# Recurrence gates multiplied ahead of the recurrent attention, ScalarE's chain between its value products, selected attention's loads issued under it

## What is computed

```python
# 1: recurrent attention (mLSTM), 4 heads of 96: q, k, v, output gate, input and forget gates
s   = einsum('bhtd,bhsd->bhts', q, k) * exp(d_log - m_t)
h   = num / maximum(abs(den), exp(-m_t));  h = rmsnorm(h) * gain * sigmoid(output gate)
# 2: gated linear recurrence (RG-LRU), 384 channels, 6 blocks of 64, over a causal convolution x of 4 taps
r, i = sigmoid(x @ w_a + b_a), sigmoid(x @ w_x + b_x)
log_a = -8 * r * softplus(-lam);  a = exp(log_a)
u = sqrt(-expm1(2 * log_a)) * (i * x)
h_t = a_t * h_{t-1} + u_t;  out = h * gelu(g)
# 3: selected attention, 4 heads of 64: each query attends to its 256 best-scored keys
softmax(q k^T / 8 + mask) v
```

## Time and profile before

| | us |
|---|---|
| median of 3 runs | 3240.03 (3236.83 to 3241.76) |
| the profiled execution | 3239.98 |
| its span, first to last instruction | 3238.4 |
| TensorE busy | 3015.8 (93%) |
| VectorE busy | 1597.6 (49%) |
| ScalarE busy | 1195.7 (37%) |
| GpSimd busy | 1042.3 (32%) |
| TensorE, mean granted clock | 0.969 of full |

### The profile page before, as it was taken

How to read it: one execution, slowest core, us unless ns; L and a number is a source line. 1 busy time by engine, 2 the same in 40 slices (tenths; PEclk the granted TensorE clock), 3 DMA queues, 4 the chain that set the end, 5 groups by cost and what they waited for, 6 DMA issues and landing times.

```text
span 3238.4 us, 49889 instructions
## 1 busy us (share of the span) xinstructions
PE 3015.8 (93%) x18148; PEld 2596.6 (80%) x18148; DVE 1597.6 (49%) x3075; ACT 1195.7 (37%) x2173; POOL 1042.3 (32%) x686
## 2 busy tenths in 40 slices
PE   5798976999999999998999999999999889999999
PEld 4487954777888888877999977997896889988877
DVE  2699923723222323123008377981213837878861
ACT  3311136433212221123114356772322637666750
POOL 1132201232322224564225203344331543432325
PEclk9899997899999999999999999999999999999999
DMA  2122241232111112342268533323335762231223
GB/s 96 56 97 96 89 117 39 59 112 104 46 52 45 52 45 79 116 153 107 94 139 258 141 103 79 68 82 117 141 118 185 211 167 63 84 85 40 61 96 129
DMA packets 224150, 325.68 MB, mean 101 GB/s; under 512 B 81318, under 2 KB 167206, under 8 KB 221814
## 3 DMA queue, kind: packets, MB, share of 16 engines
q1 hardware_dynamic: 188838, 277.29, 28.9%
q10 hardware_dynamic: 33360, 39.98, 3.5%
q0 software_dynamic: 1792, 6.29, 0.7%
HBM read 229.95 MB, written 93.57 MB: 100 GB/s over the span
## 4 chain that ended last, share of the span: by engine, by line
PE 71%; DVE 6%; ACT 3%; issue 2%; POOL 2%; DMA 0%; POOLq 0%; DVEq 0%; ACTq 0%
PE psum L474 15%; PE psum L2197 15%; PE psum L2400 7%; PE psum L1986 7%; PE psum L1056 6%; PE psum L1025 6%; PE psum L1036 5%; PE psum L739 2%; PE psum L716 2%; DVE arena L2798 1%; PE psum L728 1%; PE psum L1071 1%; POOL out_ring L1976 1%; PE psum L3136 1%; PE psum L2837 1%
## 5 line engine op out<-in xcount | busy, mean ns | idle before, releaser
L2197 PE MATMUL psum<-parts_ffn 128*128 128x512 f32 x2112 | 482.9, 391 | 3.6 <-DVE parts_ffn L2154 3.6
L2197 PEld LDWEIGHTS psum<-parts_ffn 128*128 128x128 f32 x2112 | 398.8, 189 | 87.4 <-issue 2.2
L474 PE MATMUL psum<-parts_even,parts_ffn 128*128 128x256 f32 x2496 | 306.1, 285 | 5.2 <-DVE parts_ffn L2534 4.0
L474 PEld LDWEIGHTS psum<-parts_even,parts_ffn 128*128 128x128 f32 x2496 | 303.9, 194 | 5.9 <-DVE parts_ffn L2534 4.5
L474 PE MATMUL psum<-parts_odd 128*128 128x248 f32 x2304 | 277.1, 283 | 19.1 <-ACT arena L514 16.7
L474 PEld LDWEIGHTS psum<-parts_odd 128*128 128x128 f32 x2304 | 273.6, 193 | 21.8 <-ACT arena L514 15.6
L2267 DVE SCALAR_TENSOR_TENSOR arena<-psum,arena 128x1023 f32<-128x1023 f32 x88 | 112.9, 1283 | 329.8 <-ACT arena L2251 323.6
L514 ACT ACTIVATE arena<-psum 128x256 f32<-128x256 f32 (+2 forms) x240 | 87.6, 376 | 456.1 <-PE psum L474 451.2
L403 PE MATMUL psum<-parts_mixer 128*128 128x512 f32 x912 | 212.1, 395 | 10.5 <-ACTq L412 10.5
L403 PEld LDWEIGHTS psum<-parts_mixer 128*128 128x128 f32 x912 | 174.5, 192 | 48.3 <-ACTq L412 7.6
L1098 ACT ACTIVATE both<-psum 128x512 fp32r<-128x512 f32 x256 | 140.1, 596 | 108.0 <-PE psum L1036 107.5
(11 more groups left out here) (339 smaller groups left out, 5848.9 us busy)
## 6 DMA issues: line engine op xcount, KB each, us to landing
arena<-ffn_up_b SPq DMA_DIRECT2D x44, 512.0 KB, 3.2
arena<-ffn_down_k SPq DMA_DIRECT2D x44, 512.0 KB, 3.6
arena<-x SPq DMA_DIRECT2D x10, 2048.0 KB, 8.6
arena<-w_in_e SPq DMA_DIRECT2D x13, 1024.0 KB, 6.7
e_tokens<-arena ACTq DMA_DIRECT2D x26, 512.0 KB, 3.1
x<-arena SPq DMA_DIRECT2D x24, 512.0 KB, 5.0
arena<-w_in_o SPq DMA_DIRECT2D x12, 992.0 KB, 6.3
o_tokens<-arena ACTq DMA_DIRECT2D x24, 496.0 KB, 3.0
```

What stands on the lines that cost most here:

```text
L474: last = pe.matmul(self.bank(t), self.hT[:, a, k, t * P:(t + 1) * P], self.weights.parts[:, self.weights.slot(s), b, k, :], start=(k, a, b ...
L2197: last = pe.matmul(self.core.psum[:, 4 * u + 2 * s + h, :], parts[:, s, a, k, :], self.hT[:, b, k, h * HALF:(h + 1) * HALF], start=(k, a, ...
```

## The change

It does the following.

- The gate products (`lru_gates`) and the sigmoids (`sigmoid_pairs`) stand ahead of the recurrent attention, as soon as `tok1`'s sums are taken out; the recurrent attention's TensorE part waits for the sigmoids. `coefficients` moves with them.
- The softplus is split off and stands between `feat1` and `tok1` on ScalarE.
- Exp, Tanh, Sqrt and Gelu, three of each, stand one by one between ScalarE's copies of value products: behind copies 4 to 6 and 12 to 14 of the two rounds. ScalarE's loop over the rounds is written out for that.
- `gate_input` follows the masks on GpSimd.
- `dsa`'s loads wait for the last applied weights of the recurrent attention only. Its q and k lie where the recurrent attention's were, and scores contract over the 64 partitions that hold data, with nothing zeroed.
- The output gates' loads stand in SyncE's queue behind `dsa`'s first loads.
- The pieces in `dsa` stand at other steps.

```diff
-        self.loads_after, self.ahead = after, None
+        self.loads_after, self.ahead, self.before_second = after, None, None
@@ Attention.sync
         for i in range(self.rounds):
+            if i == 1 and self.before_second is not None:
+                self.before_second(sp)
@@ Lru
-    def sigmoids_and_roots(self, act):
-        F = self.F
+    def softplus(self, act):
         link = Chain(act, self.act_order)
 
         link(act.activation(self.t0, self.lam, ACT.Abs))
         link(act.activation(self.t0, self.t0, ACT.Exp, scale=-1.0))
         act.activation(self.t0, self.t0, ACT.Ln, bias=1.0).then_inc(self.coef_ln, 1)
-        for f in range(F):
+
+    def sigmoid_pairs(self, act):
+        for f in range(self.F):
             act.wait_ge(self.gated, f + 1)
             act.activation(self.r[:, f], self.both(f, 0), ACT.Sigmoid, bias=self.b_a[:, f:f + 1]).then_inc(self.sigmoids, 1)
             act.activation(self.i[:, f], self.both(f, 1), ACT.Sigmoid, bias=self.b_x[:, f:f + 1]).then_inc(self.sigmoids, 1)
...
+    def decay(self, act, f):
+        act.wait_ge(self.coef_ready, 2)
+        act.wait_ge(self.sigmoids, 2 * self.F)
+
+        act.wait_ge(self.conved, f + 1)
+        act.activation(self.x[:, f], self.r[:, f], ACT.Exp, scale=self.coef2[:, f:f + 1]).then_inc(self.decayed, 1)
+
+    def half_angle(self, act, f):
+        act.wait_ge(self.decayed, f + 1)
+        act.activation(self.r[:, f], self.r[:, f], ACT.Tanh, scale=self.coef[:, f:f + 1]).then_inc(self.tanhed, 1)
+
+    def root(self, act, f):
+        act.wait_ge(self.tanhed, f + 1)
+        act.activation(self.u[:, f], self.r[:, f], ACT.Sqrt, scale=-4.0).then_inc(self.rooted, 1)
+
+    def gelu(self, act, f):
         act.wait_ge(self.g_loaded, 16)
-        for f in range(F):
-            act.activation(self.g[:, f], self.g[:, f], ACT.Gelu_apprx_tanh).then_inc(self.gelued, 1)
+        act.activation(self.g[:, f], self.g[:, f], ACT.Gelu_apprx_tanh).then_inc(self.gelued, 1)
@@ Mlstm.weigh
                 act.wait_ge(self.summed, N * i + N + n + 1)
-                act.activation(self.num[:, bass.ds(i + 2 * s, 1), t, :].rearrange("p a b -> p (a b)"), ps[:, 4 + n % 4, 0:DH + 1], ACT.Copy).then_inc(self.taken, 1)
+                act.activation(self.num[:, i + 2 * s, t, :], ps[:, 4 + n % 4, 0:DH + 1], ACT.Copy).then_inc(self.taken, 1)
+                if (i, n) in self.between:
+                    self.between[i, n](act)
@@ dense_attention
-    qs, ks, vs = core.take(2, S), core.take(2, S), core.take(2, TT, dv)
-    qp, kp = qs, (ks, ks)
+    qs, ks = core.take(2, S), core.take(2, S)
+    if rest_at is not None:
+        core.parts_top = rest_at
+    vs = core.take(2, TT, dv)
+    qp, kp = qs[0:dq], (ks[0:dq], ks[0:dq])
...
-    zeros = [qs[dq:P].rearrange("p a b -> p (a b)"), ks[dq:P].rearrange("p a b -> p (a b)")] if dq < P and not split else []
+    zeros = []
@@ build
+        softplus_part = add(Part())
...
-            hold(pe, [(mlstm.multiplied, 3 * mlstm.N), (mlstm.taken, 4 + 2 * mlstm.N)])
+            hold(pe, [(mlstm.columns_ready, 1)] + tok1.taken_out + tok1.multiplied)
             lru.make_gates(pe)
 
+        def lru_softplus(act):
+
+            hold(act, scores.done)
+            lru.softplus(act)
+
         def lru_sigmoids(act):
 
-            hold(act, [(mlstm.columns_turned, 1), (mlstm.rows_stored, 16)])
-            lru.sigmoids_and_roots(act)
-
+            hold(act, [(mlstm.columns_turned, 1), (mlstm.rows_stored, 16)] + tok1.weights.raw_free())
+            lru.sigmoid_pairs(act)
...
-            hold(pe, [(mlstm.columns_ready, 1)] + tok1.taken_out)
+            hold(pe, [(mlstm.columns_ready, 1)] + lru.gates_done)
             mlstm.multiply(pe)
 
+        for f in range(lru.F):
+            for i, n, step in ((0, 4 + f, lru.decay), (0, 12 + f, lru.half_angle), (1, 4 + f, lru.root), (1, 12 + f, lru.gelu)):
+                mlstm.between[i, n] = lambda act, f=f, step=step: step(act, f)
+        add(Part(tensor=lru_gates, scalar=lru_sigmoids, vector=lru.coefficients))
         add(Part(sync=mlstm_loads, tensor=mlstm_products, scalar=mlstm.weigh, vector=mlstm.apply_weights, gpsimd=mlstm_masks))
-        add(Part(tensor=lru_gates, scalar=lru_sigmoids, gpsimd=lru.gate_input, vector=lru.coefficients))
-
-        add(Part(sync=mlstm.load_output_gate))
-        vector_pieces = {0: mlstm.divide, 5: mlstm.means, 10: mlstm.normalize}
-        for h in range(mlstm.H):
-            vector_pieces[12 + h] = lambda dve, h=h: mlstm.gate(dve, h)
-        scalar_pieces = {0: mlstm.absolutes, 2: mlstm.output_gates, 3: mlstm.squares, 8: mlstm.roots}
+        add(Part(gpsimd=lru.gate_input))
+
+        vector_pieces = {4: mlstm.divide, 12: mlstm.means, 15: mlstm.normalize}
+        for h, at in enumerate((19, 20, 21, 22)):
+            vector_pieces[at] = lambda dve, h=h: mlstm.gate(dve, h)
+        recurrence_at = (5, 6, 7, 11, 13, 14)
+        scalar_pieces = {3: mlstm.absolutes, 6: mlstm.squares, 8: mlstm.output_gates, 13: mlstm.roots}
...
-            elif at > 0:
-                next(recurrence[0], None)
+            if at in recurrence_at:
+                next(recurrence[0])
...
-        core.top, core.parts_top = core.words, 11 * S
+        core.top, core.parts_top = core.words - 8, mlstm.heads_at
         dsa = dense_attention(core, "dsa", 4, 64, 64, feat[AQ:AQ + 256], feat[AK:AK + 256], tok[:, AV:AV + 256],
                                ds, mlstm.loop_done + choose.done + lru.gates_done, masks=masks, scale=64 ** -0.5,
-                              aside=(dsa_scalar_aside, dsa_vector_aside))
+                              aside=(dsa_scalar_aside, dsa_vector_aside), rest_at=11 * S)
+        assert core.parts_top <= mlstm.ends_at
+        dsa.loads_after = [(mlstm.multiplied, 3 * mlstm.N)]
...
         add(dsa)
+        dsa.before_second = mlstm.load_output_gate
```

More of the change, by code:

```diff
@@ L1278, in sigmoids_and_roots @@
             act.activation(self.i[:, f], self.both(f, 1), ACT.Sigmoid, bias=self.b_x[:, f:f + 1]).then_inc(self.sigmoids, 1)
+    def decay(self, act, f):
         act.wait_ge(self.coef_ready, 2)
-        act.wait_ge(self.sigmoids, 2 * F)
-        for f in range(F):
-            act.wait_ge(self.conved, f + 1)
-            act.activation(self.x[:, f], self.r[:, f], ACT.Exp, scale=self.coef2[:, f:f + 1]).then_inc(self.decayed, 1)
-        act.wait_ge(self.decayed, F)
-        for f in range(F):
-            act.activation(self.r[:, f], self.r[:, f], ACT.Tanh, scale=self.coef[:, f:f + 1]).then_inc(self.tanhed, 1)
-        act.wait_ge(self.tanhed, F)
-        for f in range(F):
-            act.activation(self.u[:, f], self.r[:, f], ACT.Sqrt, scale=-4.0).then_inc(self.rooted, 1)
+        act.wait_ge(self.sigmoids, 2 * self.F)
[8 more added lines that the diff above has]
+    def gelu(self, act, f):
         act.wait_ge(self.g_loaded, 16)
-        for f in range(F):
-            act.activation(self.g[:, f], self.g[:, f], ACT.Gelu_apprx_tanh).then_inc(self.gelued, 1)
+        act.activation(self.g[:, f], self.g[:, f], ACT.Gelu_apprx_tanh).then_inc(self.gelued, 1)
     def coefficients(self, dve):
@@ L1354, in __init__ @@
         self.ready_to_load = []
+        self.between = {}
         s = core.sem
@@ L1383, in place @@
         self.pt = core.take_parts(2, self.offset[TT])
-        core.parts_top = base
+        self.heads_at = base
+        self.den, self.ss = shaped(core.parts[:, base + 4 * S:base + 4 * S + 2 * H * TT], (2, H * TT))[:, 0], shaped(core.parts[:, base + 4 * S:base + 4 * S + 2 * H * TT], (2, H * TT))[:, 1]
+        core.parts_top = self.ends_at = 18 * S
         self.og, self.hn = core.take_parts(H, TT, DH), core.take_parts(H, TT, DH)
         self.sq = shaped(num[:, 0:H * TT * DH], (H, TT, DH))
-        self.den, self.ss = core.take_parts(H * TT), core.take_parts(H * TT)
-        core.parts_top = max(core.parts_top, base + 3 * 2 * S + 2 * TT * (DH + 1))
     def load_gates(self, sp):
@@ L1491, in weigh @@
         act.wait_ge(self.columns_ready, 1)
-        with act.Fori(0, 2) as i:
+        for i in range(2):
             for n in range(N):
@@ L1498, in weigh @@
                 act.wait_ge(self.multiplied, N * i + n + N - 1)
+                at = (i + 2 * s) * TT + j
                 act.activation(self.w[:, n % 2, 0:S - j * P], self.ab[:, s, j * P:S], ACT.Exp,
-                               bias=self.cs[:, bass.ds((i + 2 * s) * TT + j, 1)]).then_inc(self.weighed, 1)
+                               bias=self.cs[:, at:at + 1]).then_inc(self.weighed, 1)
             for n in range(N):
@@ L2575, in dense_attention @@
 def dense_attention(core, name, heads, dq, dv, q, k, v, out_sb, after, masks=None, scale=1.0, kv_of_slot=False,
-                    v_step=None, v_first=0, v_shared=False, aside=(None, None), split=False):
+                    v_step=None, v_first=0, v_shared=False, aside=(None, None), split=False, rest_at=None):
     half = heads // 2
-    qs, ks, vs = core.take(2, S), core.take(2, S), core.take(2, TT, dv)
```

(3 more changed lines are left out.)

1 line of the change is left out of this document (added).

## The result

The changed kernel takes **3269.23 us** (median of 20 executions, 3237.01 to 3277.18) where the kernel before takes 3240.04 (20 executions, 3236.83 to 3246.97). The ratio is 1.008, with a 95% interval of 1.0064 to 1.0096: slower by 29 us, where 29.4 us of gain were forecast. The executions of the changed kernel differ in how long TensorE's clock stays at half: in most of them the mean granted clock is 0.951 to 0.955 and the time 3265 to 3277, in three of them it is 0.961 to 0.965 and the time 3237 to 3249. The profiled execution (3271.28 us, span 3269.7, clock 0.953) is one of the many.

The account below looks back on a forecast made before the run. It took TensorE, busy for 93% of the span, as the bound and sought its idle time. Selected attention starting 25.9 us earlier and itself 3.5 us shorter made 29.4 us: 3239.98 - 29.4 = 3210.6 us, range 3204 to 3219.

Parts of the forecast that it names:

- The scores then contract over 64 partitions, which no row here has ... I take no change.: Selected attention's scores: 64 partitions in place of 128 were taken to cost nothing, from 0.43 us per 512 columns over 96.
- half clock through both rounds: Rival in the selected attention: lightly loaded TensorE lacks full clock even in the second round, +44 us, 3255; chance 0.03 (slower).
- the two are level, so 10.6 us of products leave the path and cost nothing.: Ahead of the recurrent attention: last sigmoid at 435.9, DMA wait before until 436.03, so the moved gate products hide.
- its clock should still be full: Start of the recurrent attention: TensorE stands still only 2.3 us, not 13.51, keeping full clock; gain 1.2 us.
- the forecast's 73.4: Time from the recurrent attention's first score to the selected attention's first score: 73.4 us, where before it was 99.26.
- The rival on SyncE's queue: Early selected-attention loads stand behind something on SyncE's queue, leaving only the ordering: about 3235 to 3240; chance 0.05.
- a chain in front that is late: Rival ahead of the recurrent attention: gates, sigmoids and table together late by 0 to 6 us, 3212 to 3217; chance 0.07.
- ScalarE's chain between the copies, 0.35 us: Recurrent attention's value products: activations and table loads fit between ScalarE's copies, except the last copy comes 0.35 us late.
- Softplus, coefficients, input product: 0: Softplus in ScalarE's idle time between projections, coefficients early, input product on GpSimd under value products: no cost forecast.
- The loads: Selected attention's loads issued about 493.4, head 0 there before 500, start at 509.4 in place of 535.29.
- The table switch at the start: Ahead of the recurrent attention: ScalarE loads Exp's table in 1.28 us after the last sigmoid, first weighting at 437.2.
- The selected attention, 116.2 us: Whole selected attention: 86.5 us without pieces, 26.6 for VectorE pieces, 1.9 and 0.2 on ScalarE, 1 for the clock.

Follow-up runs that it names:

- experiment 4: Changed kernel with scores over 128 partitions (upper 64 zeroed on GpSimd) and the recurrent attention's head loads released ahead of the gate products: 3214.9 us, ratio 0.9918.
- experiment 1: Changed kernel with the selected attention's scores over all 128 partitions, the upper 64 zeroed on GpSimd under the value products: 3225.49 us, ratio 0.9953.
- experiment 2: Kernel before the change with one edit, the selected attention's scores over 64 partitions: 3285.77 us, ratio 1.0126.
- experiment 3: Changed kernel with TensorE releasing the recurrent attention's head loads ahead of the gate products, not behind the sigmoids: 3262.52 us, ratio 1.0059.
- experiment 8: As experiment 4, with three extra products of unused result behind the gate products, in TensorE's wait for the sigmoids: 3212.09 us, ratio 0.9917.
- 6: As experiment 4, with the pieces in the selected attention at the steps of the kernel before: 3212.38 us, ratio 0.9913.
- 5: As experiment 4, but the selected attention's scores contract over 96 partitions, 32 of them zeroed: 3219.03 us, ratio 0.9935.
- experiment 9: As experiment 8, with the pieces in the selected attention at the steps of the kernel before: 3212.38 us, ratio 0.991.

## Why the prediction was wrong

**The step that failed first: "The scores then contract over 64 partitions, which no row here has ... I take no change."** The row it was nearest to, 96 partitions in 0.43 us for 512 columns, is right about one product: at full clock, four products of 256 columns took 1.10 us over 64 partitions (517.42 in the changed kernel) and 1.10 us over 128 (512.49 in experiment 4). The price lay in the clock of the engine, which runs everything else too: 50.0 us in D to O, 48.9 of it undone by experiment 1. The unknown was costed at one value, nothing, with no upper end. The upper end was at hand, in the rival "half clock through both rounds" (+44 us). That rival happened, a little larger (+50), but its condition was another: it was argued from how lightly TensorE is loaded, with the clock of 1.00 from 608.9 against it. That row held for scores over 128 partitions, and the change took just that away. A row of before speaks against a rival only while the change leaves alone what made the row.

The Trainium skill, TensorE: Matmul & The Clock Gate, section Why this matters for your kernels, says that a single matmul over 32 rows takes as long as one over all 128; the two rows of 1.10 us, for 64 and 128, agree. Its Part 1 says that the clock is granted by how busy TensorE is; in experiment 2 TensorE was busy for all of the 70 us from 620 to 690 and was granted 0.50, so here the trace doesn't agree: busy time as the profile counts it wasn't enough.

**The second: "the two are level, so 10.6 us of products leave the path and cost nothing."** The chain itself was sized well: products from 1.67 us after T (forecast 1.7), last sigmoid ended at 433.68, 14.9 us after T (forecast 14.5). The cover was not there. The loads that were to hide it were released by TensorE, from behind the products: 10.2 us lost. The prediction named one condition for the heads, "SyncE can't issue the heads before the projection is stored". In the trace of before the other one, TensorE's release, cost nothing, because TensorE was idle when it gave it. The prediction asked who waits for TensorE's new wait and named only TensorE's own work. Experiment 3 gave back 8.5 us of it, experiment 4 9.4.

**The third, a small one: "its clock should still be full".** In experiment 4 TensorE stood still for 2.60 us; the clock fell 0.2 us before it resumed and stayed at 0.50 for 6.7 us behind that. The mean of 0.68 over 14.6 us was read as leaving "the full clock for the first 5 us of it", which is right for the kernel before. But there the clock fell 4.1 us after TensorE had stopped, and in experiments 3 and 4 it fell 2.3 and 2.5 us after, so the 5 us (1.2 of them TensorE's own work) couldn't be carried over. Ahead of the second round some kernels lost it again. The table sets the time of M to D against how long the clock was at half in it, from windows of 0.5 us:

| | wait ahead of round 1, 2 (us) | half clock in round 1, 2 (us) | M to D (us) |
|---|---|---|---|
| 8 | none, 0.55 | 0, 0 | 71.69 |
| 1 | 12.31, 0.53 | 4.0, 0 | 72.93 |
| changed kernel | 12.18, 1.23 | 4.2, 0 | 73.73 |
| 6 | 2.60, 1.29 | 6.8, 0 | 75.08 |
| 3 | 3.50, 1.46 | 5.7, 3.4 | 76.23 |
| 5 | 2.60, 1.49 | 6.8, 3.4 | 76.79 |
| 4 | 2.60, 1.98 | 6.7, 3.4 | 77.24 |

Experiment 9 had no half clock either, and 71.23. So the forecast's 73.4 was too much for a full clock, by 1.7 to 2.2 us (it put the gain of the full clock at 1.2 us; in experiment 8 the value products ended 71.0 us after M, where before it was 73.8). The changed kernel met 73.4 because 4.2 us of half clock and a wait of 1.23 us at the second round made that up: the number came out by luck.

**Slips in its numbers.** The rival on SyncE's queue has a chance of 0.05 and a time of 3235 to 3240, but "within" has 0.03. And a chain in front that is late by 0 us gives 3210.6, not the 3212 at which that rival starts. Neither matters for the outcome.

**What was right.**

- *ScalarE's chain between the copies, 0.35 us.* The second round's 144 value products ran in one piece (16.22 us), the last copy followed 0.03 us behind, and the first score 0.69 us behind the last product. The low end, taken because the gaps were in the rows, was right.
- *Softplus, coefficients, input product: 0.* The input product ran on GpSimd from 500.99, under the value products, and nobody waited for it.
- *The loads:* issued from 501.38, 0.3 us after VectorE's last weights (501.06) and 16.0 us ahead of D, as forecast (493.4 for 509.4), and the first score waits for no DMA. The rival that they stand behind something on SyncE's queue didn't come true.
- *The table switch at the start:* in experiment 4 the last sigmoid ended at 434.80, the load took 1.28 us from 434.82 and the first weighting began at 436.12, 1.32 us after the sigmoid (forecast 1.3). With the clock full, in experiment 8, VectorE's first product came at 438.00, 3.1 us after the last sigmoid, as forecast (435.9 to 439.0); in experiment 4 it waited for TensorE at half clock and came 4.35 us after. The Trainium skill, ScalarE: Activation LUTs, section What ACT_TABLE_LOAD costs, adds a drain to each switch, 1.4 us; the trace doesn't agree, as in experiment 4 there are 0.02 us in front of the load and 0.02 behind it.
- *The selected attention, 116.2 us, with 128 partitions:* 120.86, 119.45 and 118.62 in experiments 1, 4 and 8, and at the old steps 115.79 and 118.20 in 6 and 9. At the steps that the forecast was made for it is thus 2.4 to 4.7 us over; whether that is the rival of the clock in the thin steps isn't shown.
- *The split on GpSimd, 10 us of slack.* In experiment 4 it is freed at 603.69, and with its 18.1 us is done at 621.8, 10.1 ahead of O.

In experiment 9 the whole stretch took 204.98 us, against 204.2 by the forecast's sum. That is near by luck in part: T to M is 0.9 us over the forecast, M to D 2.2 under and D to O 2.0 over, in a kernel with 128 partitions, early heads, three added products and the old steps.

## What to carry to other kernels

When work is put ahead of a wait to hide it, look for who raises the semaphore that starts the transfer waited for: if it is the same engine, from behind the moved work, the wait moves along. And on TensorE don't cut a contraction from 128 to 64 partitions to save a memset without looking at the granted clock: zeroed partitions cost this kernel nothing on the path, and their absence cost 50 us.

## What the runs showed of the hardware that was not expected

TensorE stayed at half clock while busy nearly the whole time: in the changed kernel 0.51 over the 169.6 us from 517.4 to 687 (busy for 168.5 of them), in experiment 2 0.50 from 533 to 690 (busy for all of the last 130), with scores over 64 partitions between transposes and value products over 128. With 96 partitions the same order was granted 0.99 in the second round, with 128 1.00. In experiment 3's profiled execution the full clock came back from 590 on and stayed, though the scores still had 64 partitions; by their times and mean clocks (0.961 to 0.965) something of the kind happened in three of the changed kernel's 20. Why in those and not in the others stays open.

The clock can still be full in a short gap and be lost around its end. It fell 0.2 us before TensorE resumed after 2.60 us (experiment 4), and about 0.7 us after it had resumed from gaps of 1.46 and 1.98 us at the second round (experiments 3 and 4). The length of the gap doesn't decide alone: the clock was lost after 1.46 and 1.49 us (experiments 3 and 5) and kept after 1.51 us in the kernel before and 1.78 us in experiment 2. It also took longer to come back after a short stop, 6.7 us after 2.60 us of standing still (experiment 4), than after a long one, 4.2 us after 12.18 us (the changed kernel). Three otherwise useless products of 2.74 us together in the first gap shortened the stage behind it, M to D, to 71.2 and 71.7 us, from 75.1 and 77.2.
